# A streaming encoder layer: gate projection in 512-column blocks of half the rows, and threshold counts divided between two engines

## What is computed

```
h = x @ w_in                        # (2048 + 8*16) tokens x 1024 -> 5720 columns
z_s, xbc, dtr, q, k, v, z_a, qi, ki, wi = split(h)
y_ssd = ssd(silu(causal_conv(xbc)), dt, ...) gated by silu(z_s)
score = relu(qi . ki) weighted by wi, masked by chunk       # per query
top_val, top_idx = top_k(score, 256)                        # 132 for the sampled tokens
att = softmax(q . k[top_idx] - alibi) @ v[top_idx] * silu(z_a)
y = LayerNorm(ALPHA * x + concat(y_ssd, att) @ w_out)
```

## Time and profile before

| | us |
|---|---|
| median of 3 runs | 2738.84 (2737.27 to 2738.99) |
| the profiled execution, its own time | 2742.46 |
| its span in the profile | 2740.6 |
| PE busy in the span | 2525.7 |
| DVE, ACT, POOL busy | 2095.4, 1090.0, 741.6 |
| `stage_project`, first matmul to the next stage | 362.26 to 1385.30 |

### The profile page before, as it was taken

The page is one execution under the profiler, slowest core; times in us unless marked ns, Lnnn a source line. Parts: engine busy times, 40 slices in busy tenths (PEclk is TensorE's granted clock), DMA queues, the critical chain, the costliest instruction groups (busy, mean ns, idle before and its releaser), DMA issues. The chain is left out here.

```text
span 2740.6 us, 39432 instructions
## 1 busy us (share of the span) xinstructions
PE 2525.7 (92%) x14787; PEld 2196.2 (80%) x14787; DVE 2095.4 (76%) x3434; ACT 1090.0 (40%) x2163; POOL 741.6 (27%) x779
## 2 busy tenths in 40 slices
PE   7998969999999999998989967999999988899997
PEld 6887859999999788998966645777777777788886
DVE  3799799999999999999868855777776667444443
ACT  3678621112122122213455644655555555222221
POOL 0010323233333233334636763322121021000000
PEclk9999989999999999999999978999999999999998
DMA  7330062332235333347744543211110046422210
GB/s 248 108 97 4 1 222 78 94 94 89 83 93 174 111 97 95 98 141 233 216 129 161 170 156 96 83 58 49 43 43 24 20 146 238 149 93 92 93 62 23
DMA packets 187480, 294.70 MB, mean 108 GB/s; under 512 B 29451, under 2 KB 131734, under 8 KB 185751
## 3 DMA queue, kind: packets, MB, share of 16 engines
q1 hardware_dynamic: 164489, 220.30, 25.6%
q0 software_dynamic: 22800, 71.88, 7.4%
HBM read 181.92 MB, written 110.20 MB: 107 GB/s over the span
## 5 line engine op out<-in xcount | busy, mean ns | idle before, releaser
L863 DVE TENSOR_SCALAR_CACHE_REDUCE project_junk<-all_S,project_cand 128x528 bf16<-128x528 f32 (+7 forms) x256 | 370.0, 1445 | 1.1
L766 PE MATMUL PS<-project_xh,project_wh 128*128 128x384 f32 (+1 forms) x880 | 317.2, 360 | 34.3 <-DMA project_xl<-x_parts 34.3
L766 PE MATMUL PS<-project_wh,project_xh 128*128 128x256 f32 x1224 | 347.8, 284 | 0.0
L766 PE MATMUL PS<-project_wl,project_xh 128*128 128x256 f32 x1224 | 346.8, 283 | 0.0
L766 PE MATMUL PS<-project_wh,project_xl 128*128 128x256 f32 x1224 | 346.8, 283 | 0.0
L2262 DVE TENSOR_TENSOR attend_ptl<-PS,attend_pth 128x512 fp32r<-128x512 f32 x272 | 185.2, 688 | 172.0 <-ACT attend_pth L2124 171.3
L766 PE MATMUL PS<-project_xh,project_wl 128*128 128x384 f32 (+1 forms) x880 | 316.2, 359 | 0.0
L766 PE MATMUL PS<-project_xl,project_wh 128*128 128x384 f32 (+1 forms) x880 | 315.9, 359 | 0.0
L863 DVE TENSOR_SCALAR_CACHE_REDUCE project_tie<-all_S,project_cand 128x384 bf16<-128x384 f32 (+6 forms) x224 | 315.7, 1409 | 0.0
L766 PEld LDWEIGHTS PS<-project_wh,project_xh 128*128 128x128 f32 x1224 | 235.4, 192 | 0.0
L766 PEld LDWEIGHTS PS<-project_wl,project_xh 128*128 128x128 f32 x1224 | 235.4, 192 | 0.0
(11 more groups left out here) (333 smaller groups left out, 5690.8 us busy)
## 6 DMA issues: line engine op xcount, KB each, us to landing
project_raw<-in_w_in SPq DMA_DIRECT2D x80, 512.0 KB, 4.3
featT<-project_st POOLq DMA_DIRECT2D x66, 192.0 KB, 2.1
all_S<-featT SPq DMA_DIRECT2D x12, 1024.0 KB, 5.6
featT<-project_st POOLq DMA_DIRECT2D x44, 256.0 KB, 2.3
x_parts<-index_s_x POOLq DMA_DIRECT2D x10, 1024.0 KB, 7.3
gate_s<-project_st POOLq DMA_DIRECT2D x68, 128.0 KB, 2.2
gate_a<-project_st POOLq DMA_DIRECT2D x68, 128.0 KB, 2.6
ssd_x<-x_tok SPq DMA_DIRECT2D x17, 512.0 KB, 4.9
```

What stands on the lines that cost most here:

```text
L766: last = nc.tensor.matmul(PS[:, r % 8, 0:w], lhsT, rhs, start=(k == 0 and j == 0), stop=(k == KT - 1 and j == 2))
L863: v.tensor_scalar((junk, tie)[j % 2][:, 0:L], tile_scores(j), th, None, op, ALU.add, accum_out=into[:, j:j + 1]).then_inc(counted, 1)
```

## The change

- **Gates.** Blocks 11 to 18 of a half become pairs: each block holds 4 of the 8 row groups of 512 columns (`pair`). A "p" unit (128 tokens x 512 columns) needs both blocks of a pair. PE does the first half (12 matmuls of width 512) of six tiles into six banks (`part`), then whole units of the other tiles in the two other banks (`loose`), then the rest of the six. "x" units go between them through the loose banks, one or two at a time.
- **First blocks.** In each half the four features of blocks 0 and 1 are made for the first cut of x, then for the next ones.
- **Counts.** The six widest tiles (15 to 10, `SUM`) are only compared on VectorE (into `junk` and `tie` in turn), and ACT sums the result with an activation that accumulates. VectorE keeps the nine others as before (`DIRECT`). A compare waits until the sum of two compares earlier is done, and a pass ends when all its sums are. Where ACT does its sums is fixed beforehand: between the evictions, by a clock that adds up assumed durations of the units and gives a pass 19.0 us.
- **Places.** `silu_at` is 30 + 4.0f, counted over all gates and values of the second half (72 steps) instead of the last 40 units, where it was 4.5 + 3.7f. All masks are stored behind block 35's weights.

```diff
+        outs, used, steps = [], [], []
+        bank, freed, last_in = [], [], {}
+        LATE = (len(cols) - NF) * (HALF[1][1] - HALF[1][0])
+        silu_at = [int(30 + 4.0 * f) for f in range(NF2)]
         turn_at = [silu_at[f] + 3 for f in range(XF)]
         GRP = [(4 * j, min(4, TILES + 1 - 4 * j)) for j in range(5)]
         silu_before, turned_by = {}, []
-        late = 0
+        late, turn = 0, []
...
+        def passed(k, loose):
+            nonlocal late, odd
+            if not hf:
+                return
+            for _ in range(k):
+                late += 1
+                for f in range(NF2):
+                    if silu_at[f] == late:
+                        silu_before.setdefault(len(outs), []).append(f)
+                for f in range(XF):
+                    if turn_at[f] == late or late == LATE and turn_at[f] > late:
+                        turn.extend((f, g0, kk) for g0, kk in GRP)
+            for _ in range(len(turn) if late == LATE else min(len(turn), k + (len(turn) > 4))):
+                odd += 1
+                turn_one(loose[odd % 2] if loose else None)
...
+                if n == 0:
+                    for c0, w in even_pieces((t1 - t0) * P):
+                        for f in range(4):
+                            steps.append((unit((hf, f // 2, "f", f, c0, w)), "all"))
+                    used.append(len(outs) - 2)
...
+            part = [(bank[-1] + 1 + j) % 8 for j in range(6)]
+            loose = [(bank[-1] + 7 + j) % 8 for j in range(2)]
+            for n in range(NF, NF + 8, 2):
+                split, whole = range(t0, t0 + 6), range(t0 + 6, t1)
+                ahead = []
+                for t in split:
+                    ahead.append(len(steps))
+                    steps.append(None)
+                    passed(1, loose)
+                for t in whole:
+                    odd += 1
+                    steps.append((unit((hf, n, "p", t, 0, 4 * P), loose[odd % 2]), "all"))
+                    passed(2, loose)
+                used.append(len(outs))
+                for j, t in enumerate(split):
+                    r = unit((hf, n, "p", t, 0, 4 * P), part[j])
+                    steps[ahead[j]] = (r, "first")
+                    steps.append((r, "rest"))
+                    passed(1, loose)
+                used.append(len(outs))
+            bank_next = loose[0]
...
+        SUM = [SEL.index(t) for t in range(TILES - 1, 9, -1)]
+        WIDE, SLIM = [SEL.index(t) for t in (9, 8, 7, 6)], [SEL.index(t) for t in (5, 4, 3, 2, ST)]
+        DIRECT = [SLIM[i // 2] if i % 2 == 0 else WIDE[i // 2] for i in range(len(WIDE) + len(SLIM))]
+        assert len(SUM) + len(DIRECT) == NSEL and keys_of(9) + keys_of(5) <= SEQ
+        PASSES, PASS_US = 33, 19.0
+        sums_before, at, todo = {}, 0.0, 0
+        for r, (_, _, kind, _, _, w) in enumerate(outs):
+            at += {"f": w * 24 * 0.00045, "t": 2.9, "x": 0.45, "p": 5.45}[kind]
+            n = 0
+            while (todo < PASSES * len(SUM)
+                   and todo // len(SUM) * PASS_US + todo % len(SUM) * 2.4 + 3.0 <= at):
+                todo, n = todo + 1, n + 1
+            sums_before[r] = n
...
+                        if NF <= n < NF + 8:
+                            q = (n - NF) % 2
+                            dst = raw[:, kh].rearrange("p (k i) c -> p k (i c)", i=2)
+                            own = b.w_rows[:, 4 * q + 2 * kh:4 * q + 2 * kh + 2, cols[n - q]:cols[n - q] + 4 * P]
+                        else:
+                            dst, own = raw[:, kh], b.w_rows[:, 4 * kh:4 * kh + 4, cols[n]:cols[n] + 2 * P]
+                        sp.dma_start(dst, own).then_inc(raw_in[kh], 16)
                     if blk == NBLK - 5:
+                        store_masks(LOWS, mask_st[0])
...
+                    need = own + 1 if kind == "p" and share != "first" else own
+                    if need > blk:
+                        blk = need
+                        pe.wait_ge(w_hi, 2 * blk + 2)
+                        pe.wait_ge(w_lo, 2 * blk + 2)
...
+                        for q in range(q, q + sums_before[r]):
+                            j, rows = SUM[q % len(SUM)], (junk, tie)[q % 2]
+                            L, into = keys_of(SEL[j]), above if q // len(SUM) == PASSES - 1 else count
+                            act.wait_ge(compared, q + 1)
+                            ac(rows[:, 0:L], rows[:, 0:L], ACT.Copy, accum_out=into[:, j:j + 1]).then_inc(summed, 1)
+                        q += 1 if sums_before[r] else 0
...
+                    def compare(i):
+                        q, j = n * len(SUM) + i, SUM[i]
+                        wait(dve, summed, q - 1)
+                        v.tensor_scalar((junk, tie)[q % 2][:, 0:keys_of(SEL[j])], tile_scores(j), bound(j), None, op
+                                        ).then_inc(compared, 1)
+                    def direct(i):
+                        q, j = n * len(DIRECT) + i, DIRECT[i]
                         L = keys_of(SEL[j])
-                        th = against if isinstance(against, float) else against[:, j:j + 1]
-                        v.tensor_scalar((junk, tie)[j % 2][:, 0:L], tile_scores(j), th, None, op, ALU.add,
+                        o = keys_of(9) if j in SLIM else 0
+                        wait(dve, counted, q - 1)
+                        v.tensor_scalar(spare[:, o:o + L], tile_scores(j), bound(j), None, op, ALU.add,
                                         accum_out=into[:, j:j + 1]).then_inc(counted, 1)
+                    for i in range(len(DIRECT)):
+                        if i < len(SUM):
+                            compare(i)
+                        direct(i)
+                    dve.wait_ge(counted, (n + 1) * len(DIRECT))
+                    dve.wait_ge(summed, (n + 1) * len(SUM))
```

More of the change, by code:

```diff
@@ L668, in stage_project, with unit, turn_one @@
-        NBLK = len(used)
-        silu_last = [f for f in range(NF2) if f not in silu_before.values()]
+        late, turn = 0, []
+        def unit(o, at=None):
+            r = len(outs)
+            outs.append(o)
+            bank.append((bank[-1] + 1) % 8 if at is None and bank else at or 0)
+            freed.append(last_in.get(bank[r], -1) + 1)
+            last_in[bank[r]] = r
+            return r
+        def turn_one(at):
+            f, g0, k = turn.pop(0)
+            steps.append((unit((hf, n, "x", f, g0 * P, k * P), at), "all"))
+            if g0 == GRP[-1][0]:
+                turned_by.append(len(outs))
@@ new lines, in stage_project @@
+        odd = 0
+        for hf, (t0, t1) in enumerate(HALF):
+            for n in range(2):
+                if n == 0:
[3 more added lines that the diff above has]
+                    used.append(len(outs) - 2)
+                else:
+                    used.append(len(outs))
+            for n in range(2, NF):
+                for f in (2 * n, 2 * n + 1):
+                    for c0, w in even_pieces((t1 - t0) * P):
+                        steps.append((unit((hf, n, "f", f, c0, w)), "all"))
+                used.append(len(outs))
+            part = [(bank[-1] + 1 + j) % 8 for j in range(6)]
[17 more added lines that the diff above has]
+                    passed(1, loose)
+                used.append(len(outs))
+            bank_next = loose[0]
+            for t in range(t0, t1):
+                steps.append((unit((hf, NF + 8, "t", t, 0, 2 * P), bank_next), "all"))
+                bank_next = None
+                n = NF + 8
+                passed(1, None)
+            used.append(len(outs))
@@ L671, in place @@
+        assert todo == PASSES * len(SUM)
+        silu_last = [f for f in range(NF2) if f not in [g for some in silu_before.values() for g in some]]
         def place(o):
@@ new lines, in _ @@
+                blk = -1
+                for r, share in steps:
+                    hf, n, kind, i, c0, w = outs[r]
+                    own = hf * len(cols) + n
+                    if share != "rest":
+                        wait(pe, proj_out, freed[r])
+                    if kind == "x":
+                        pe.wait_ge(silu_done, i + 1)
+                        for k in range(w // P):
+                            last = nc.tensor.transpose(PS[:, bank[r], k * P:(k + 1) * P],
+                                                       acc[i % 3][:, c0 + k * P:c0 + (k + 1) * P], b.ident[:, :])
+                        last.then_inc(proj, 1)
+                        continue
+                    need = own + 1 if kind == "p" and share != "first" else own
[3 more added lines that the diff above has]
+                        pe.wait_ge(w_lo, 2 * blk + 2)
+                    if n == 0 and i == 0:
+                        k = [c for c, _ in even_pieces((HALF[hf][1] - HALF[hf][0]) * P)].index(c0)
+                        pe.wait_ge(x_in[k], 32 * (hf + 1))
+                    for k in {"all": range(KT), "first": range(KT // 2), "rest": range(KT // 2, KT)}[share]:
+                        for j, (a, x) in enumerate(PARTS):
```

(11 more changed lines are left out.)

87 lines of the change are left out of this document (16 added, 71 removed).

## The result

| | before | after |
|---|---|---|
| median of 4 runs, us | 2738.91 (2737.27 to 2739.13) | 2715.44 (2711.76 to 2719.87) |
| ratio, 95% interval | 1 | 0.9918 (0.9905 to 0.9932) |
| the profiled execution, its span | 2740.6 | 2709.9 |
| second half's first gate matmul | 1133.44 | 1119.35 |
| last projection matmul | 1379.15 | 1352.32 |

The change makes the kernel 0.8% faster, 23.5 us. The forecast was 2688, 51 us, and its range ended at 2713: the direction is right, the size is less than half, and the time lies outside the range.

The account below looks back on a forecast made before the run. PE was taken as the first bound, with the search costing time through lateness at the stage's end. Terms -11.9 - 10.6 - 10.6 - 4 + 7 - 20.7 = -50.8 put the span at 2689.8, the median at 2688, range 2670 to 2713.

Parts of the forecast that it names:

- First blocks: Start of the stage: four units use the first cut of x, so PE skips the second cut's wait; -10.6 us.
- Gate matmuls: Gates of both halves: a 512-column unit costs 5.405 us against two of 2.868, saving 0.331; -11.9 and -10.6 us.
- ACT's order in the gates: First half's gates: ACT's sums delay evictions and `low`, so PE stands at pairs 2 and 3; +7 us, between 0 and 20.
- Between the halves: Seam before second features: PE waits about 6 us for x, 3 for the clock; 9 in place of 13.2, -4 us.
- which I put 8 us late below: Seam: assumed lateness of ACT's evictions, behind which block 21's weights and then the load of x stand.
- The walk's own 13 us: First half's gates: stepping through ACT's list put the first pair's last eviction at about T+62, 13 us late.
- The search: Passes held to ACT's clock of 19 us; search ends near 1000 instead of 1103.26, masks near 1127.
- The first rival: Search: POOL holds compares, so passes take 20 to 20.5 us; 15 to 30 us less gain, 2703 to 2718; chance 0.18.
- The end of the stage: Last part: of 23.7 us lost, all but 3 for evictions waiting for store buffers are regained; -20.7 us.
- The 23.7: Second half's gates to stage end before the change: us lost beyond pure matmul time and transposes, 18.1 idle, the rest clock.
- the third: Last part: convolution still late behind masks and stores, or transposes wait for two loose banks; 2703 to 2709; chance 0.10.
- The signs: Profile marks named beforehand: first value unit near 841, passes of 19, search end near 1000, stage end near 1334.

Follow-up runs that it names:

- Experiment 4: Changed kernel with the clock of ACT's list of sums following PE's real order of split units (the corrected list): 2695.85 us, 0.9858.
- experiment 3: Kernel before with only the order of the first blocks changed: 2727.50 us, 0.9974.
- experiment 6: Changed kernel with corrected list of sums, plus masks' stores and tokens' loads two blocks earlier in SP's order: 2694.49 us.
- experiment 9: Kernel before with eight store buffers in the last part instead of four, nothing else: 0.9979 (0.9957 to 1.0002).
- experiments 8: Changed kernel with eight store buffers in the last part instead of four, its list of sums kept: 2706.96 us, 0.9895.
- 7: Changed kernel with corrected list of sums, plus eight store buffers in the last part instead of four: 2684.52 us, 0.9808.
- experiment 11: Changed kernel with corrected list, eight store buffers, and second half's gates as 256-column blocks on a ring of eight banks: 2684.07 us.
- 12: Changed kernel with corrected list, eight store buffers, and masks' stores and tokens' loads two blocks earlier: 2684.43 us.
- the three with the ring and four buffers: Changed kernel with 256-column gates on eight banks: both halves, 2706.53 us; same with corrected list, 2707.52; corrected list, second half alone, 2694.18.

## Why the prediction was wrong, step by step

| term | predicted | measured |
|---|---|---|
| start of the stage | 0 | -1.1 |
| first blocks | -10.6 | -10.7 |
| gates and values, first half, with stops | -11.9 + 7 | -3.4 |
| between the halves and second features | -4 | +1.1 |
| last part (gates -10.6, lateness -20.7) | -31.3 | -12.7 |
| behind it | 0 | -3.9 |
| sum | -50.8 | -30.7 |

The measured column is the difference of the two profiles, cut at the first and last matmuls of each kind of unit.

- *Gate matmuls*: the price was taken from 222 matmuls in 50 us; 0.2267 apiece makes a unit 5.44, not 5.405. The price of the old unit was low too, 2.88 and not 2.868, since the window ended 1.25 us before block 19 did. A wide unit saves 0.32 and not 0.331, so 68 x 0.011 = 0.7 us are missing. A count in a window takes in both its ends; the distance of starts is the price.
- *First blocks*: right, size and place.
- *ACT's order in the gates*: right in mechanism and size. The last eviction of the first pair was 12.2 us late (13 predicted), stops at pairs 2 and 3 and none at 4, ended by `low`, 8.3 lost (7 predicted). Within it, pair 2 cost less (1.9, where 4 to 5 were predicted) and pair 3 more (3.2 for 2). Experiment 4 shows that this list is their cause.
- *Between the halves*: the step "which I put 8 us late below" failed. The walk's own 13 us held at the fourth pair too: the rounding stood at 855.51, x was issued at 861.85, PE waited 10.4 and not 6, with its clock at 0.82 from 868 to 896. The seam was also priced too high before: with the units at 5.44 and block 19 ending at 883.25 it cost 250.2 - 44 x 5.44 = 10.8 us and not 13.2, and 251.25 - 239.4 = 11.9 after (9 predicted). 5 us off. The first blocks alone (experiment 3), without split units, bring 9 us here (871.30 to 1112.40), and with the corrected list the pairs have them too (861.57 to 1102.75): the list took them back.
- *The search*: it ended at 1008 (predicted near 1000) and the masks at 1138 (1127). The first 13 passes, from 380.42 to 630.03, took 19.2 us on average (15.6 to 22.5), close to ACT's 19.0, and experiment 6, in which the first convolution starts at 1129.5 and not at 1173.6, has no shorter last part. The first rival, a long pass, is no part of the miss. POOL's hold on compares is there as forecast, one compare of 1920 beside `low`, 5.07 us where it takes 1.22 alone (DVE and POOL in order of time):

```profile
726.80 5.07 DVE L953 TENSOR_SCALAR project_tie<-all_S,project_cand 128x1920 bf16<-128x1920 f32 x1
...
726.09 4.76 POOL L919 TENSOR_TENSOR project_wl<-project_raw,project_wh 128x1024 fp32r<-128x1024 f32 x2
```

  By the Trainium skill, page "SBUF — State Buffer", section "Who interferes with whom", a `tensor_scalar` without accumulator output can be blocked for the length of a GpSimd instruction; this trace agrees.
- *The end of the stage*: this is the step that failed, 18.6 of the 20.1 us. "I leave 3 us for evictions that wait for a store buffer" was a guess with no row behind it. Of the 12.7 us that the part did get shorter 10.2 are matmuls; the lost time there went only from 24 to 21 us. What was forecast of the convolution came true: PE's waits for silus, 17.5 us, went to none. Two things were wrong. The 23.7 were booked as convolution alone, though 8.4 of them were store buffers by the profile of experiment 9, and with these half of PE's wait for silus; some 15 are left for the late search. And what the changed kernel loses was not counted: 10 to 12 us for four store buffers (experiments 8 and 7), where 3 were left, and some 9 for the form of the pairs in this part, two loose banks (experiment 11), where nothing was.
- *The rivals*: the third, the end does not get its gain, is what happened, by one of its two mechanisms (transposes and loose banks; tokens behind masks were refuted by experiment 6) and one that it did not name, the store buffers. It had 0.10 and a time of 2703 to 2709; with the seam and the matmuls' price, 5 + 0.7, it would have reached 2715.
- *The signs*: most of those that were named came true (the first value unit at 842 for 841, no wait at the second cut of x, stops at pairs 2 and 3 ended by `low`, none over 5 us behind 1200, none behind silus), and the time was still wrong: the stage's projection ended at 1352. Two passes took 32.5 and 28.4 us, at the first and the third pair, where ACT stood in its list. The signs test the mechanisms that the forecast knew; none of them watched the evictions of the last part.

## What to carry to other kernels

When a change takes away the wait that ends last, the gain is bounded by what waits next: list, for the same stretch, every engine's own waits (here ACT's for its stores, 54 us, were in the trace of before, unused) and price the second one before booking the first. An order that is fixed beforehand by a clock must be computed from the order in which work is really done; where PE splits units and the clock did not, one list cost 17 us in two places. Wider units need the buffers of what consumes them, and here a form that leaves two banks to small and whole units took back 9.4 of the 10.2 us that its wide matmuls saved. A wait for X names only the last link: half of PE's wait for silus went away with buffers that no silu uses.

## What the hardware showed besides

- A store of 256 KB took 2.4 (gate_s) and 2.6 us (gate_a) from issue to landing in the median over the whole run, but 3.4 (gate_a) and 4.6 (x_tok) in the last part, where the DMA engines are busy for 0.63 and five evictions of a transposed tile come close together. The medians of DMA issues from 1200 to 1350:

```profile
x_tok<-project_st POOLq DMA_DIRECT2D x32, 256.0 KB, 4.6
gate_a<-project_st POOLq DMA_DIRECT2D x16, 256.0 KB, 3.4
```

- The kernel before ran between 2718.85 and 2741.83 us in the 15 executions beside experiments 8, 9, 11 and 12, and within 2 us in the first 4. A difference of 0.2% is not told by such a group. The last part's length in the profile was 233.0, 233.6 and 233.5 in three kernels with pairs and four buffers, within 0.6 us; but it was 229.0, 230.8 and 236.9 in the three with the ring and four buffers, each from one execution, so it is not always the finer measure.
